# Hybrid decoder step: the last expert tile's lower part moved ahead of four value tiles' on VectorE

## The reference, cut to what matters

```python
hid = jnp.einsum("thkd,td->thk", u_tab[eidx], xt)
a = g * jax.nn.gelu(hid, approximate=False)
return jnp.einsum("thk,thkd->td", a, v_tab[eidx])
```

## Time and profile before

| | us |
|---|---|
| three runs, median | 1804.65 |
| lowest, highest | 1803.26, 1804.83 |
| profiled execution, whole | 1799.53 |
| its span, first to last instruction | 1798.0 |

### The profile page before, as it was taken

The page is one execution under the profiler, slowest core; times in us unless marked ns, Lnnn a source line. Parts: engine busy times, 40 slices in busy tenths (PEclk is TensorE's granted clock), DMA queues, the critical chain, the costliest instruction groups (busy, mean ns, idle before and its releaser), DMA issues.

```text
span 1798.0 us, 30227 instructions
## 1 busy us (share of the span) xinstructions
PE 1689.9 (94%) x9914; PEld 1493.1 (83%) x9914; DVE 1403.2 (78%) x3186; ACT 764.0 (42%) x1194; POOL 582.2 (32%) x513
## 2 busy tenths in 40 slices
PE   5999998789899999989999999997999999999997
PEld 4999743449799998989999999996888888888885
DVE  3235366434399999969998999997898999999998
ACT  3223144222434432346675677663333333333333
POOL 0000460000254543564422424433333333333331
PEclk9999998889899999999999999998999999999999
DMA  3344551361243332459999999999999999999995
GB/s 116 100 160 145 156 170 42 131 229 58 74 156 107 133 118 76 158 201 367 396 348 319 391 372 358 412 394 369 382 386 388 384 383 385 389 384 383 385 388 185
DMA packets 195265, 470.85 MB, mean 262 GB/s; under 512 B 17970, under 2 KB 100530, under 8 KB 192606
## 3 DMA queue, kind: packets, MB, share of 16 engines
q1 hardware_dynamic: 134430, 254.46, 40.2%
q0 software_dynamic: 50944, 178.96, 26.3%
q10 hardware_dynamic: 9792, 36.18, 5.1%
HBM read 411.97 MB, written 61.32 MB: 263 GB/s over the span
## 4 chain that ended last, share of the span: by engine, by line
PE 43%; DVE 23%; issue 5%; DMA 2%; ACT 0%; DVEq 0%; SPq 0%; ACTq 0%; POOLq 0%
PE va L233 10%; PE va L231 10%; PE va L232 10%; PE hp L231 4%; PE hp L232 4%; PE hp L233 4%; PE ggp L1867 3%; DVE gathered L1471 2%; DVE og L1923 2%; DVE ulo L1947 2%; DVE vw L1471 1%; DVE eq L1730 1%; DVE sc L1682 1%; DVE X L1689 1%; DVE X L1681 1%
## 5 line engine op out<-in xcount | busy, mean ns | idle before, releaser
L231 PE MATMUL hp<-mid_hi,uhi 128*128 128x384 f32 x1024 | 360.1, 352 | 28.8 <-DVE ulo L1947 18.7
L232 PE MATMUL hp<-mid_lo,uhi 128*128 128x384 f32 x1024 | 348.9, 341 | 0.0
L233 PE MATMUL hp<-mid_hi,ulo 128*128 128x384 f32 x1024 | 347.8, 340 | 0.0
L232 PE MATMUL va<-vlo,ahi 128*128 128x512 f32 x768 | 298.8, 389 | 0.0
L231 PE MATMUL va<-vhi,ahi 128*128 128x512 f32 x768 | 298.8, 389 | 0.0
L233 PE MATMUL va<-vhi,alo 128*128 128x512 f32 x768 | 298.8, 389 | 0.0
L1805 POOL DMA_INDIRECT gathered<-in_v_experts,idx_row x160 | 189.2, 1183 | 331.8 <-DVEq L2250 270.9
L231 PEld LDWEIGHTS hp<-mid_hi,uhi 128*128 128x128 f32 x1024 | 195.9, 191 | 34.7 <-DVE ulo L1947 21.6
L1383 POOL TENSOR_TENSOR ulo<-uw,uhi 128x1024 fp32r<-128x1024 f32 x49 | 123.2, 2514 | 271.3 <-ACT uhi L1379 271.2
L1813 ACT ACTIVATE vhi<-vw 128x1024 fp32r<-128x1024 f32 x128 | 134.8, 1053 | 155.3 <-DMA vw<-in_v_experts 153.1
L232 PEld LDWEIGHTS hp<-mid_lo,uhi 128*128 128x128 f32 x1024 | 196.3, 192 | 0.0
(11 more groups left out here) (337 smaller groups left out, 3374.8 us busy)
## 6 DMA issues: line engine op xcount, KB each, us to landing
uw<-in_u_experts SPq DMA_DIRECT2D x128, 512.0 KB, 5.9
vw<-in_v_experts SPq DMA_DIRECT2D x128, 512.0 KB, 10.5
gate_matrix<-gst ACTq DMA_DIRECT2D x12, 2048.0 KB, 11.8
hidden_values<-gelu_out SPq DMA_DIRECT2D x72, 192.0 KB, 7.9
hd<-hidden_values SPq DMA_DIRECT2D x16, 768.0 KB, 9.6
gt<-gate_matrix SPq DMA_DIRECT2D x16, 768.0 KB, 13.7
uw<-hidden_values SPq DMA_DIRECT2D x16, 768.0 KB, 9.6
uw<-gate_matrix SPq DMA_DIRECT2D x16, 768.0 KB, 13.6
```

The lines of the kernel that those rows point to most:

```text
L231: nc.tensor.matmul(out, a_hi, b_hi, start=first, stop=False)
L232: nc.tensor.matmul(out, a_hi, b_lo, start=False, stop=False)
L233: return nc.tensor.matmul(out, a_lo, b_hi, start=False, stop=last)
```

## The change

The wait for the stored gates and the loop over four `rest_of_v` leave pass e = 4 and stand behind the tail loop. The last `ulo` (pass e = 5) thereby comes ahead of the four `vlo`. Passes 6 and 7 of that loop have nothing on DVE.

```diff
@@ gate_on_vector, behind over_turns
                     nc.vector.tensor_copy(idx_row[:, 0:BR], eidx[:, 0:BR]).then_inc(xs["idx"], BR)
                     dve.sem_inc(xs["fetched"], ROW)
-                    dve.wait_ge(stored[1], 16 * (NI + 1))
-                    for c in range(GT):
-                        rest_of_v(dve, c, c)
+            dve.wait_ge(stored[1], 16 * (NI + 1))
+            for c in range(GT):
+                rest_of_v(dve, c, c)
             dve.wait_ge(gs["act"], 1)
             nc.vector.tensor_tensor(coef[:], hid[:], sgate[:], ALU.mult)
```

## The result

The changed kernel is slower by a little: ratio to the kernel before 1.0037, 95% interval 1.0025 to 1.0049 (medians 1809.5 us over 8 runs and 1803.34 us over 8 runs). In a second set of runs the ratio was 1.0023 (1.0013 to 1.0034). The prediction of no change (1804.9, range 1802.0 to 1807.4) missed it.

What follows compares the result with a forecast made beforehand. The prediction took the value stage as bound by the DMA-fed supply, with PE following. At the end -0.2 us (PE's earliness) and +0.4 us (supply shift) gave +0.2 us, 1804.9 us on the median, range 1802.0 to 1807.4.

Steps and rivals of the forecast that it cites:

- PE's wait ahead of tile 127: Ahead of the last expert tile PE would wait 1.0 us instead of 5.55, with its clock staying full.
- Value tile 0: PE would start the value stage at 1258.3 instead of 1262.46, 4.2 us earlier, behind a new wait of 2.7 us.
- The supply's start: At the value stage's start, `crow` would come at 1260.6, 4.3 us earlier, following the gelu of tile 127 on ACT.
- The gates' issue: SyncE's load of the gates for value tiles 4 to 7 would leave some 0.4 us later.
- The gates' landing: Gates of value tiles 4 to 7 would land 15.1 us after issue as before, at 1271.6 instead of 1271.2.
- d: Shift of the value stage's supply, which counts for the end: between -1.0 and +1.14 us, taken as +0.4.
- rival C: Clock falls in the new 2.7 us wait; PE loses some 2.3 us, the end nothing; included in the forecast's 0.66.
- Rival B: Earlier row requests make gates of tiles 4 to 7 land 2.7 us later, at 1274.3; end 1807.3 us; chance 0.15.
- The value stage is bound by what the DMA engines supply: In the value stage the DMA engines have no free time at 385 GB/s; PE follows the supply.
- the forecast's own range: Shift of the end by -0.2 plus (-1.0 to 1.14) us, giving 1803.4 to 1805.6 us.

Runs made afterwards that it cites:

- run 1: The changed kernel, but GpSimd asks for the second index row's five gathers only after the gates of tiles 4 to 7 landed; ratio 1.0022 to before.
- run 3: The changed kernel, but SyncE issues the final gain and gates of tiles 8 to 11 only after those of tiles 4 to 7 landed; ratio 1.0020.
- run 4: The changed kernel, but SyncE loads hidden values and gates of tiles 4 to 7 ahead of the four `vw` loads; ratio 0.9998 to the kernel before.
- run 10: The changed kernel, with the start of the adds put off by a wait and five small memsets; ratio 0.9995 to the kernel before.
- 5: The changed kernel, but `crow` waits for the high part of `vw` of tile 4, so the adds start later; ratio 1.0005 to the kernel before.
- run 8: The kernel of run 4, with half the columns of every `vw` load from value tile 8 on left out; ratio 0.9984 to the kernel before.
- 11: The kernel of run 10, with the final gain and gates of tiles 8 to 11 held until those of tiles 4 to 7 landed; ratio 1.0014.
- run 12: The changed kernel run and profiled again, with nothing further changed; ratio 1.0023 to the kernel before.
- run 7: The kernel before, with half the columns of every `vw` load from value tile 8 on left out; ratio 0.9999 to the kernel before.

## Why the prediction was wrong, point by point

- **PE's wait ahead of tile 127**: forecast 1.0 us, measured 1.02, and the clock stayed full. Right.
- **Value tile 0**: forecast 4.2 us earlier behind a wait of 2.7, measured 12.78 - 8.60 = 4.2 behind 2.72. Right.
- **The supply's start**: forecast `crow` at 1260.6, 10.9 us behind the copy, measured 10.9. The size is right, but the reason that was given is in part luck: the sum followed only ACT, and POOL's clearing of `acc_s` was the later of the two.
- **The gates' issue**: forecast 0.4 us later, measured 7.07 against 6.44 us behind the copy, 0.6. Small miss.
- **The gates' landing**: this is the step that failed. The sum took 15.1 us over unchanged, while two paragraphs on it moved DVE's adds, and with them GpSimd's row requests, 4.3 us forward (measured: `crow` at 10.9 instead of 15.2, the first request at 13.2 instead of 17.5). The duration held for a transfer that had the engines to itself for its last microseconds. Measured 22.5.
- **The lower and the upper bound of d**, -1.0 and +1.14: wrong with it. The `weigh` of tile 4 shifted by 29.57 - 22.92 = +6.7 us, and the shift of the supply at the stage's end, d, was 534.4 - 529.4 = +5.0 us where +0.4 was taken:

```profile
1787.22 0.55 DVE L1825 TENSOR_TENSOR alo<-uw,ahi 128x384 fp32r<-128x384 f32 x1
```

  The argument was that busy engines only reorder bytes. They don't stay busy: DVE stood still, no buffer came free, nothing was asked for, and in 1290 to 1300 the engines had holes. Two stretches after, in the same columns as the earlier trace rows, where four tiles of the stage before show 1.06 and 385:

```profile
1294.00:1296.00 2.00, 2.00 (x10) 1.66 (x9) 1.85 (x2) 1.02 (x2) 0.33 (x1) 1.00 0.93 272
...
1298.00:1300.00 2.00, 2.00 (x10) 1.65 (x10) 2.00 (x4) 1.43 (x2) 1.05 (x2) 1.00 0.69 178
```

- **The size of the loss.** PE needs tile 4 at 29.1 us behind the copy before (1278.8) and got it at 33.3: 4.2 us. The wait also dropped the clock:

```profile
1284.00:1288.00 4.00, 1.84 (x4) 1.49 (x5) 3.85 (x6) 1.94 (x3) 1.15 (x1) 0.50 1.05 300
```

  0.50 is the 1.2 GHz level. From tile 4 to the last matmul's start it takes 507.4 us instead of 505.7, 1.7 more. 4.2 + 1.7 = 5.9, which is the 5.8 of the whole within the rounding. After the stall PE has no wait left, so it sets the end, and the point of rival C, that a drop of the clock costs nothing since the supply sets the end, did not hold for this later drop. The 2.7 us wait itself was followed by a granted clock of 0.55 and 0.60 in 1262 to 1266, so C came true too. It cost 1.7 us of PE's lead, and in this kernel nothing at the end, as PE then waited for tile 4 anyway. Whether C comes true is not settled by the wait: the same 2.7 us stood ahead of tile 0 in all nine profiles with the new order, the clock fell in five of them (first, 1, 3, 4, 10) and stayed full in four (5, 8, 11, 12). Here it is in run 12, which is the changed kernel again; the third figure from the end is the granted clock:

```profile
1263.00:1267.00 4.00, 3.67 (x16) 3.08 (x17) 2.98 (x7) 1.72 (x3) 2.18 (x3) 1.00 0.98 344
```

- **Rival B** named the right mechanism, place and deciding point: rows ahead of the gates, landing later than 1272.6 (22.9 behind the copy). It was mis-sized: 2.7 us for two rows, where the landing took 7.4 us more and all five rows had landed at about the same time as the gates. It also got only 0.15, since I held that bytes moved earlier need not be moved later, which is the argument that failed under d.
- **The value stage is bound by what the DMA engines supply**: right, by runs 4, 7, 8 and 10. In the two runs with full loads in which the gates came in time, a start 4.2 us earlier changed the end by -0.4 us (run 4) and +0.2 us (run 10); with less to move (run 8 against run 7) it came 3.0 us earlier. Both ends lie inside the forecast's own range of -1.2 to +0.9 us. The Trainium skill, page "Perfetto Trace Analysis", section "Optimization Strategies", advises to speed up what PE waits for; here that wait was real, and its removal was worth at most 0.4 us at the end (run 4), since the supply had the next claim. The 435 GB/s of the page "DMA: Bandwidth & Descriptors", section "Specifications", was not reached in the value stage: before and after it moved 385 GB/s over 1300 to 1700, and in its best stretches of 2 us 418.

## What to carry to other kernels

When an edit lets an engine run earlier, follow what that engine frees, and so which transfers will be asked for earlier, and look whose landing time was read in a gap that these will now fill. A landing time in a trace belongs to the traffic beside it, and is no constant of the transfer. The load that an engine will need next should be asked for first, ahead of those that are needed later (run 4), and not be protected by holding back the others until it is through (run 1).

## What the runs showed of the hardware that was not expected

- Nearly finished is not landed. In run 3 a few hundredths of the 3.67 MB of SyncE's queue were left at 26 us, and the gates landed 3.4 us later.
- Two queues that were both full shared the engines by packets and not by bytes in 1269 to 1273 of the changed kernel (309 and 335 packets, 1.13 and 0.50 MB), so the one with the shorter packets got the smaller part. That is one stretch, read and not tested by a run of its own.
- The same wait of 2.7 us on PE was followed by a lowered clock in five profiles and by a full one in four.
- The same program's position at one instruction, about 1250 us into it, moved between 1249.0 and 1258.5 us over the profiles, in kernels that don't differ ahead of it (1249.7 and 1258.5 for the kernel before itself), while the 548 us behind it agreed within 0.3 us (in the changed kernel, with its stall, within 1.6). The runs of the kernel before spread over 8 to 13 us in the later sets. So a difference of two spans says little here; counted from a common instruction, two profiles tell some two microseconds.
- A stall of 6.5 us on PE cost 1.7 us more through the clock than its own length.
